# Projections of a gated attention block: two of four token blocks computed by pairs of weight tiles with seven half products instead of eight

## The reference

```
h = RMSNorm(x)
[q|k|v|z_att|b|c|u|z_conv|g_att|g_conv] = h @ W_in          # 1024 -> 6144
att = diff_attention(rotary(q), rotary(k), v)               # 4 heads, causal by chunks of 64
att = rmsnorm(att) * silu(z_att);   yA = att @ W_att_out
cv  = b * conv3(c * u) * silu(z_conv);  yB = cv @ W_conv_out
m   = sigmoid(g_att + bias0) * yA + sigmoid(g_conv + bias1) * yB
out = x + RMSNorm(m @ W_out)
```

## Time and profile before

| | us |
|---|---|
| median of 3 runs | 1772.46 |
| lowest, highest | 1770.55, 1774.26 |
| the profiled execution's own time | 1767.66 |
| its span in the profile | 1765.8 |
| TensorE busy | 1741.4 |
| VectorE busy | 890.1 |
| ScalarE busy | 585.0 |
| GpSimd busy | 109.4 |

### The profile page before, as it was taken

One profiled execution on the slowest core, in us unless ns is written; L12 is line 12 of the kernel. 1 busy time (PEld: TensorE's weight loads), 2 busy tenths in 40 slices (PEclk: granted clock), 3 DMA queues, 4 the chain that ended last, 5 costly groups with the idle time before them and its releaser, 6 DMA issues.

```text
span 1765.8 us, 22477 instructions
## 1 busy us (share of the span) xinstructions
PE 1741.4 (99%) x8512; PEld 1459.0 (83%) x8512; DVE 890.1 (50%) x1895; ACT 585.0 (33%) x1040; POOL 109.4 (6%) x82
## 2 busy tenths in 40 slices
PE   7999999999999999999999999999999999999998
PEld 6888888888888888888888887888888888888887
DVE  5536334444433611267767665767766453424242
ACT  5422112121101211244444444444444442323231
POOL 0000000000000000110101112111001040000000
PEclk9999999999999999999999999999999999999999
DMA  6545746465503445975666669658576875353532
GB/s 238 150 165 224 276 167 211 170 203 179 179 24 110 153 119 145 310 230 186 198 203 207 203 212 289 193 178 229 197 226 186 273 267 186 113 179 107 185 107 72
DMA packets 164678, 328.90 MB, mean 186 GB/s; under 512 B 15569, under 2 KB 60625, under 8 KB 159185
## 3 DMA queue, kind: packets, MB, share of 16 engines
q1 hardware_dynamic: 164562, 327.38, 58.7%
HBM read 216.16 MB, written 111.16 MB: 185 GB/s over the span
## 4 chain that ended last, share of the span: by engine, by line
PE 92%; DMA 4%; DVE 1%; SPq 1%; issue 1%; ACT 1%; DVEq 0%; ACTq 0%
PE bank L970 19%; PE bank L972 19%; PE bank L971 19%; PE bank L1100 17%; PE bank L1060 5%; PE bank L1032 3%; PE bank L1033 3%; PE bank L1043 3%; DMA q_st<-qk_s 1%; DMA z_in<-z_s 1%; DMA ring<-gate_s 1%; PE bank L980 1%; PE bank L1080 1%; PE bank L1077 1%; DMA qk_s<-stage 1%
## 5 line engine op out<-in xcount | busy, mean ns | idle before, releaser
L970 PE MATMUL bank<-ht,w 128*128 128x512 f32 x896 | 348.6, 389 | 0.0
L971 PE MATMUL bank<-ht,w 128*128 128x512 f32 x896 | 348.6, 389 | 0.0
L972 PE MATMUL bank<-ht,w 128*128 128x512 f32 x896 | 348.5, 389 | 0.0
L1100 PE MATMUL bank<-ht,w 128*128 128x512 f32 x912 | 236.9, 394 | 0.0
L972 PEld LDWEIGHTS bank<-ht,w 128*128 128x128 f32 x896 | 168.2, 188 | 34.9
L971 PEld LDWEIGHTS bank<-ht,w 128*128 128x128 f32 x896 | 168.2, 188 | 34.9
L970 PEld LDWEIGHTS bank<-ht,w 128*128 128x128 f32 x896 | 168.2, 188 | 34.9
L1100 PEld LDWEIGHTS bank<-ht,w 128*128 128x128 f32 x912 | 166.3, 188 | 31.8
L1632 DVE CUSTOM_DVE_ANT_0 e<-bank,zeros 128x512 f32<-128x512 f32 x192 | 124.9, 688 | 132.6 <-PE bank L1033 132.2
L1312 ACT ACTIVATE e<-e,nbias 128x128 f32<-128x128 f32 (+15 forms) x128 | 153.7, 1201 | 69.8 <-DVE nbias L1641 69.6
L1100 PE MATMUL bank<-hx,w 128*128 128x512 f32 x576 | 153.9, 394 | 0.0
(11 more groups left out here) (140 smaller groups left out, 2507.9 us busy)
## 6 DMA issues: line engine op xcount, KB each, us to landing
w<-split_s SPq DMA_DIRECT2D x124, 512.0 KB, 4.9
split_s<-piece SPq DMA_DIRECT2D x24, 1024.0 KB, 5.0
q_st<-qk_s SPq DMA_DIRECT2D x128, 128.0 KB, 5.0
gate_s<-gate_st SPq DMA_DIRECT2D x64, 256.0 KB, 5.2
ring<-gate_s SPq DMA_DIRECT2D x64, 256.0 KB, 3.4
raw<-in_w_in SPq DMA_DIRECT2D x28, 512.0 KB, 6.1
ht_s<-ht SPq DMA_DIRECT2D x3, 4096.0 KB, 15.8
qk_s<-stage SPq DMA_DIRECT2D x48, 192.0 KB
```

The source lines that it names most:

```text
L970: nc.tensor.matmul(out, left[0], right[0], start=start, stop=False)
L971: nc.tensor.matmul(out, left[0], right[1], start=False, stop=False)
L972: return nc.tensor.matmul(out, left[1], right[0], start=False, stop=stop)
L1100: mm = nc.tensor.matmul(bank[2 + u % 2][:], unit_weights(u)[:, term // 2, k, :], h_slot(bb, k)[:, term % 2, :], start=i == 0, stop=i == PE ...
```

## The change

Blocks 0 and 1 are computed for all 28 tiles as before (two blocks per tile). For blocks 2 and 3 the tiles are taken in 14 pairs q = (2q, 2q+1). With the weights as a 2x2 matrix A of halves (tile by upper or lower four k-tiles) and the tokens as B (k half by block), the pair's four blocks come from seven products P1 to P7 (Winograd's form of Strassen's way), each of 4 k-tiles x 3 = 12 matmuls.

- The sums T1 to T4 of B are made once by GpSimd (40 operations of 128x512) and split by ScalarE and VectorE into the place of ht[0] and ht[1], which are then finished.
- The sums S1 to S4 of A are made per pair by GpSimd (4 operations of 128x512). All seven left operands are split per pair by ScalarE and VectorE (`split_a`, 128x512 each, six slots).
- Raw weights are loaded twice: once for blocks 0 and 1, again by pairs.
- P1 is copied out of PSUM by ScalarE; VectorE forms U2, U3, C22, C21 and C12 (five operations of 128x512 per pair); P2 and P3 accumulate in place.
- The first two and the last two pairs are interleaved. Pieces are now in tiles 6 to 17, the tables spread over tiles 0 to 3, the ids in tile 4, the ht stores in halves of 2 MB in tiles 1 to 6. Rotary tables are loaded by halves. The convolution's edge is carried between halves. Gates take the blocks in the order 2, 0, 1, 3.

```diff
+LINE_PAIRS = LINE // 2
+ONE_PAIR = ("P1", "P5", "P6", "P7", "P2", "P4", "P3")
+FIRST_TWO = ("P1", "P2", "P5", "P6", "P7", "P4", "P3")
+LAST_TWO = ("P5", "P6", "P1", "P7", "P4", "P2", "P3")
+X, Y = LINE_PAIRS - 2, LINE_PAIRS - 1
+PRODUCTS = ([(q, x) for x in FIRST_TWO for q in (0, 1)] + [(q, x) for q in range(2, X) for x in ONE_PAIR]
+            + [(q, x) for x in LAST_TWO for q in (X, Y)])
+A_SLOTS = 6
+H_ORDER = (2, 0, 1, 3)
...
         def pieces_at(p):
-            q = 2 * (p - CONV_P)
+            q = 2 * (p - CONV_P - 2)
             return (q, q + 1) if 0 <= q < PIECES else (None, None)
...
# SyncE
+            def load_half_pair(q, x):
+                if q == 0:
+                    sp.wait_ge(w_lo_done, LINE - 2 + x + 5)
+                    sp.wait_ge(w_hi_done, LINE - 2 + x + 5)
+                elif q == 1:
+                    sp.wait_ge(ht_stored, 16 * 2 * (NB - 1))
+                    sp.wait_ge(t_sum, 8)
+                else:
+                    sp.wait_ge(s_sum, S_POS[q - 2, "S4"] + 1)
+                    sp.wait_ge(w_lo_done, split_at(max(POS[q - 2, y] for y in ("P1", "P2", "P4"))))
+                n = tile_of(2 * q + x)
+                sp.dma_start(raw_pair[q % 2][x][:], t["w_in"][n * P:(n + 1) * P, :]).then_inc(raw_loaded[q % 2], 16)
...
-            for p in range(LINE - 2):
+            for p in range(LINE):
                 qa, qb = pieces_at(p)
                 before_tile(p)
                 if qa is not None:
                     store_piece(qa)
                     load_piece(qb)
-                for b in range(NB):
+                for b in range(2):
                     store_block(p, b)
...
# GpSimd
+            pool.wait_ge(ht_lo_done, 2 * NT)
+            pool.wait_ge(dve_done, done_at(QK_P + 1, 1))
...
+            for x in (1, 3):
+                for k in range(4):
+                    t_sums(x, k)
+            for x in ("S1", "S3"):
+                for q in (0, 1):
+                    s_sums(q, x)
+            for k in range(4):
+                t_sums(2, k)
+            for q in (0, 1):
+                s_sums(q, "S2")
+            for k in range(4):
+                t_sums(4, k)
+            for q in (0, 1):
+                s_sums(q, "S4")
+            for q in range(2, X):
+                for x in S_SUMS:
+                    s_sums(q, x)
...
# TensorE
-            for p, b in SEQ:
+            for p in range(LINE):
                 pe.wait_ge(w_hi_done, p + 5)
                 pe.wait_ge(w_lo_done, p + 5)
...
+            def product(i):
+                q, x = PRODUCTS[i]
+                base = 4 * (q % 2)
+                pe.wait_ge(w_hi_done, split_at(i))
+                pe.wait_ge(w_lo_done, split_at(i))
+                if x == "P1":
+                    out, right = bank[base + 2], ht[2][:, 0:4]
+                    if q >= 2:
+                        pe.wait_ge(dve_done, done_at(2 * q - 4, 2))
+                elif x == "P2":
+                    out, right = bank[base + 2], ht[2][:, 4:8]
+                    pe.wait_ge(p1_out, q + 1)
...
+                elif x == "P4":
+                    out, right = bank[base], ht[1][:, 4:8]
+                    pe.wait_ge(sum_done, SUM_POS[q, "U2"] + 1)
...
+                for k in range(4):
+                    if q == 0 and x in ("P5", "P6", "P7", "P4"):
+                        pe.wait_ge(ht_lo_done, 2 * NT + 4 * T_ORDER.index({"P5": 1, "P6": 2, "P7": 3, "P4": 4}[x]) + k + 1)
+                    adds = x in ("P2", "P3")
+                    hi, lo = a_slot(i)[:, 0, k, :], a_slot(i)[:, 1, k, :]
+                    nc.tensor.matmul(out[:], hi, right[:, k, 0, :], start=k == 0 and not adds, stop=False,
+                                     skip_group_check=adds)
...
# ScalarE: in each pair
+            for q in range(2, X):
+                i = POS[q, ONE_PAIR[0]]
+                take_p1(q)
+                for j in range(4):
+                    split_a(i + A_SLOTS + j)
+                split_a(i + A_SLOTS + 4)
+                put_out(2 * q, 2)
+                split_a(i + A_SLOTS + 5)
+                put_out(2 * q + 1, 2)
+                split_a(i + A_SLOTS + 6)
+                put_out(2 * q, 3)
+                put_out(2 * q + 1, 3)
...
# VectorE
+            for q in range(2, X):
+                i = POS[q, ONE_PAIR[0]] + A_SLOTS
+                split_a(i)
+                split_a(i + 1)
+                form_u2(q)
+                split_a(i + 2)
+                form_u3(q)
+                form_c22(q)
+                split_a(i + 3)
+                split_a(i + 4)
+                put_out(2 * q, 2)
+                form_c21(q)
+                split_a(i + 5)
+                put_out(2 * q + 1, 2)
+                form_c12(q)
+                split_a(i + 6)
+                put_out(2 * q, 3)
+                put_out(2 * q + 1, 3)
```

More of the change, by code:

```diff
@@ L115, in segments, with stored_to @@
     return out
-def stores_before(p):
-    return NT // 4 + sum(stores_of(x) for x in range(p))
 def stage_at(p, b):
-    return (2, 3, 0, 1)[(AT[p, b] - AT[LINE - 2, 1]) % 4] if p >= LINE - 2 else b
+    return AT[p - 1 if kind_of(p) == "conv" and place_of(p) == 3 else p, b] % 4
+def stored_to(p, i):
+    last = max(AT[x, y] for x, y in SEQ if x < p)
+    return NT // 4 + sum(stores_of(x) for x, y in SEQ[:last + 1] if stage_at(x, y) == i)
 def stored_before(p, b):
@@ L138, in done_at, with nth, nth_sigmoid, nth_hi @@
     return NT + AT[p, b] + 1
+def nth(p, b, kind, places):
+    return sum(kind_of(x) == kind and (kind == "z" or place_of(x) in places) for x, _ in SEQ[:AT[p, b] + 1])
+def nth_sigmoid(p, b):
+    return nth(p, b, "z", ()) + nth(p, b, "conv", (3,))
+def nth_hi(p, b):
+    return nth(p, b, "conv", (3,)) + nth(p, b, "qk", (0, 1, 2, 3))
+def tmp_user_before(p, b):
+    users = [(x, y) for x, y in SEQ[:AT[p, b]] if kind_of(x) == "conv" and place_of(x) == 3 and y % 2 == b % 2
+             or kind_of(x) == "qk" and place_of(x) == 0]
+    return users[-1] if users else None
+def bank_at(p, b):
+    if b < 2:
+        return 4 * (p % 2) + b
+    return 4 * (p // 2 % 2) + {(0, 2): 2, (0, 3): 3, (1, 2): 0, (1, 3): 1}[p % 2, b]
 def x_place(i):
@@ L731, in _ @@
+            sp.wait_ge(proj_done, product_at(POS[X, "P3"] - 1))
+            load_unit(3)
+            for q in (X, Y):
+                store_block(2 * q, 3)
             for c in range(BLK, S, BLK):
@@ L1013, in _ @@
                 mm.then_inc(proj_done, 1)
+            for i in range(len(PRODUCTS)):
+                product(i)
             score_bank = (0, 1, 4)
@@ new lines, in _ @@
+            i = POS[X, LAST_TWO[0]] + A_SLOTS
+            for j in range(4):
+                split_a(i + j)
+            for j, q in enumerate((X, Y)):
+                form_u2(q)
+                split_a(i + 4 + j)
+            for j, q in enumerate((X, Y)):
+                form_u3(q)
+                form_c22(q)
+                split_a(i + 6 + j)
+            for q in (X, Y):
+                put_out(2 * q + 1, 3)
+            for q in (X, Y):
+                form_c21(q)
+            for q in (X, Y):
+                put_out(2 * q + 1, 2)
```

544 lines of the change are left out of this document (418 added, 126 removed).

## The result

| | before | after |
|---|---|---|
| median, us | 1771.51 | 1855.31 |
| lowest, highest | 1770.24, 1774.26 | 1852.6, 1856.17 |
| span of the profiled execution | 1765.8 | 1853.0 |

The changed kernel is slower: ratio 1.0476 (95% interval 1.0464 to 1.0489), +83.8 us. The prediction was +44 and 1816 us, with a range up to 1844. Its direction was right and its size was not.

What follows compares the result with a forecast made beforehand. It took TensorE to bound the kernel, and the piece chain to bind under the shortened tiles. Terms -38.1 + 71 + 1 + 5 + 5 = +44 us on 1772.5 gave 1816 us, range 1794 to 1844.

Steps and rivals of the forecast that it cites:

- Products: Tile pairs over blocks 2 and 3: 168 fewer matmuls at 0.2267 us each, -38.1 us.
- Piece chain: Tiles 10 to 19: loading and splitting two weight pieces per tile through one buffer outlasts the shorter tiles; TensorE idles, +71 us.
- Clock: Rival: TensorE's clock falls in the gaps and stays low; some 25 us, so 1841; chance of the costly form 0.05.
- weaker form: TensorE's clock drops in each gap; each tile starts slow for a few us, hidden in the 6 us of idle.
- costly form: The clock stays low, a 48-matmul tile takes 20.5 us and becomes the bound; some 25 us, 1841; chance 0.05.
- T sums: Start of the pairs: GpSimd's last 16 sums race the first two pairs and T4 delays P4; +5 us.
- Steady pairs: VectorE's 11.1 and 20.6 us against 19.04 per pair; U2's slack absorbs the overhang, GpSimd's sums hidden; 0 us.
- Rotated pair: First q/k pair: four blocks' rotation keeps VectorE and ScalarE into the next pair, delaying P1's copy; +5 us (0 to 8).
- Handover: Products to attention: loads fall in the last 38 us of products, two gate units cover the last splits; 0, at worst +5.
- the two things that the prediction named as its refutation: Signs that it is wrong: piece stores come 5.4 us apart, or the idle time sits in the pairs.
- GpSimd or the two-pair start binds as well: Rival: 512-column GpSimd operations take 2.03 us or more; +14 on the start, S sums late in pairs; 1845, chance 0.12.

Runs made afterwards that it cites:

- two_raw: Kernel after with a second buffer for raw pieces, so a load waits for the split two pieces back: 1782.58 us, ratio 1.0064 to the kernel before.
- start: Kernel after with ScalarE's copies of both P1 put before the splits of S2 at the start of the pairs: 1855.83 us, ratio 1.0473.
- start2: Kernel after with start's order, T2's sums in their own buffer and the first two pairs' raw weights loaded one tile earlier: 1842.18 us, ratio 1.0385.
- rot: pair_order's kernel with pair 10's rotated blocks put off behind U2, U3 and C22 of pair 11: 1851.48 us, ratio 1.0446.
- swap: Kernel after with the two rotated q/k tiles in two different pairs and GpSimd's sums starting one tile later: 1859.13 us, ratio 1.0493.
- pair_order: Kernel after with P1's copy ahead of the last two blocks' put_out and raw weights loaded after block 2's stores: 1843.49 us, ratio 1.0404.
- all6: Kernel after with the edits of two_raw, start2 (including start) and pair_order, and the Line's store buffers renumbered: 1751.95 us, ratio 0.9890.
- all10: all6 with the last two pairs starting at P1 instead of P5: 1752.00 us, ratio 0.9889.
- all8: all6 with the rotated q/k tiles in two different pairs and GpSimd's sums a tile later, as in swap: 1760.35 us, ratio 0.9942.

## Why the prediction was wrong

- *Products, -38.1*: right. Where nothing waits, a product starts every 2.72 us.
- *Piece chain, +71*: right in its mechanism, place and size (71.5; the cycles 8.55 and 9.34 us against the 8.63 and 9.6 that I took). two_raw takes it away and gives back 73 us, so it was latency and not traffic. Only the form was off: 52.4 us are idle time, and the rest is slow matmuls behind the gaps.
- *Clock*: as the prediction's weaker form had it. The Trainium skill ("TensorE: Matmul & The Clock Gate", Part 1) states that an idle TensorE falls to half clock and regains it under work; the spacing of 0.43 us after each gap agrees. The costly form didn't occur. But the thought that the slow start hides in the idle time holds for the chain alone: behind its last gap it costs 1.6 us, and behind the three long gaps in the pairs 7.1 us, which no term of the prediction had.
- *T sums, +5*: mis-sized, 16 measured. GpSimd's sums took 1.59 to 1.75 us there, between the two ends that I had, 1.28 and 2.03; the failure was the path. I had followed T4 to P4. What bound was T2: its sums wait for T1's buffer, S2 waits behind them in GpSimd's queue, and in ScalarE's queue the copy of P1 waits behind the split of S2. I had counted each engine's work and not who stands behind a waiting instruction on its engine. start shows that the order alone gives nothing, and start2 that with T2 and the raw weights early as well nearly all of it goes.
- *Steady pairs, 0*: wrong by the same oversight, +5. I had weighed 20.6 us of VectorE work against 19.04 and let U2's slack take the overhang. The wait is at P2, for ScalarE's copy of P1 behind the put_out of the pair before.
- *Rotated pair, +5 (0 to 8)*: +19, the step that failed furthest. Its first 7 us are the mechanism that I named. I had not followed SyncE: the raw weights of pair 13 are issued behind pair 10's stores, and four engines wait in a row for them. And the wait for VectorE's rotations doesn't end with the pair; in the runs with other orders it comes out before P3 (rot, swap), before P5 of the next pairs (pair_order, all6), or behind the last product (all10).
- *Handover, 0 (at worst +5)*: +8.1, for a buffer that two stages share. I had looked at loads and splits and not at which stage buffer the last block falls on.

The sum missed by 40 us by the medians, of which the pairs are 31 and the handover 8. One of the two things that the prediction named as its refutation is met: idle time sits in the pairs too. The rival "GpSimd or the two-pair start binds as well" (1845, chance 0.12) was nearest. It had the start at +19, where 16 was measured, but for GpSimd operations of 2.03 us or more. They took 1.59 to 1.75, and the waits came from the order; that its number is near is luck.

## What to carry to other kernels

When a stage's matmul time is cut, each engine's work in the new, shorter period is only the first bound. Then write out for each engine, in its queue's order, which instruction waits for what, and look for a short operation that TensorE needs (a copy, a sum, a load) behind a long wait of a neighbour. Before two stages of one length are priced apart, ask what one buffer forces to be serial: here a second 512 KB buffer was worth 73 us, and of the algorithm's 38 us the time showed 4 once five edits had taken such waits away, and 19 with seven.

A wait that ends can uncover others that cost as much (start: 11.5 us gone, nothing gained), so waits at one place are removed together, and a kernel with all of them removed is run.

## What the runs showed of the hardware that was not expected

- GpSimd and VectorE slow each other where both read SBUF. GpSimd's 128x512 TENSOR_TENSOR takes 1.29 us at 490.37 and 1.65 at 499.46, between 1.59 and 1.75 up to 513 us, while VectorE's splits from SBUF go from 0.69 us to 1.16 (four in 4.66 at 498.71) and 1.71 (two in 3.42 at 510.00). VectorE's operation with one input in PSUM keeps 0.68 (503.29, beside a GpSimd sum). The Trainium skill ("SBUF — State Buffer", Who interferes with whom) states that a VectorE instruction with two SBUF inputs contends with a GpSimd instruction that reads SBUF, for ports that one of them holds exclusively, and that one with a single SBUF input doesn't; the trace agrees in who is slowed. Where both run without a pause (506.65 to 512.8), one of each takes 1.7 us, somewhat less than the 1.98 of both alone.
- A short gap of TensorE can bring the low clock. In the kernel after the matmuls stand 0.43 us apart behind gaps of 4.37 us (before 250.53) and of 2.90 (before 216.53), and 0.23 apart behind one of 2.40 (before 501.34). Gaps of one length don't always do the same: behind 2.60 us in all6 (before 671.26) five matmuls start 0.22 to 0.31 us apart and the next eight 0.39 to 0.43, behind 2.60 us in all8 (before 658.39) all stay near 0.23.
- The second buffer raised the traffic in 200 to 300 us from 238 to 347 GB/s without slowing TensorE: 100.00 of 100 us busy at clock 1.00.
